# A Conformer layer on one core: the first feed-forward part and the input projection of four token tiles laid between the attention steps of the four others

## What is computed

```
x = x + 0.5 * SwiGLU_1(RMSNorm(x))
h = RMSNorm(x); z = h @ w_in                        # 2500 columns: queries, keys, values, indexer
group A: differential attention, 4 heads, two softmaxes per head, p0 - lam * p1, 128-wide values
group B: 8 query heads over one shared key and value head; a 4-head indexer scores all keys,
         the 256 best of each query are kept (top_k), and attended
x = x + concat(A, B) @ w_out
x = x + 0.5 * SwiGLU_2(RMSNorm(x))
outputs: x of prompt and sample, and the new keys and values of both
```

## Time and profile before

| | us |
|---|---|
| median of 3 executions | 2976.89 (2973.33 to 2980.42) |
| the profiled execution | 2983.27 |
| its span | 2981.5 |
| TensorE busy | 2581.9 (87%) |
| VectorE busy | 1353.0 (45%) |
| ScalarE busy | 858.9 (29%) |
| GpSimd busy | 127.4 (4%) |
| DMA | 74 GB/s in the mean |

### The profile page before, as it was taken

The page is one execution under the profiler, slowest core; times in us unless marked ns, Lnnn a source line. Parts: engine busy times, 40 slices in busy tenths (PEclk is TensorE's granted clock), DMA queues, the critical chain, the costliest instruction groups (busy, mean ns, idle before and its releaser), DMA issues. The chain is left out here.

```text
span 2981.5 us, 35915 instructions
## 1 busy us (share of the span) xinstructions
PE 2581.9 (87%) x13666; PEld 2273.2 (76%) x13666; DVE 1353.0 (45%) x2724; ACT 858.9 (29%) x1431; POOL 127.4 (4%) x191
## 2 busy tenths in 40 slices
PE   5999999999987997357788678888999877999998
PEld 4999999999986886236565567677778666988998
DVE  5333333333325422487443377887655323444343
ACT  3111111111113111354311355653333213222221
POOL 1000000000002211001000000110000000000000
PEclk8999999999998999556889789999999988999999
DMA  5111111111002213511531623332222132221220
GB/s 184 41 43 42 43 42 43 44 42 42 5 20 94 106 43 91 186 39 43 158 107 43 176 78 92 95 85 73 71 68 60 48 126 92 84 84 42 84 84 35
DMA packets 197714, 222.02 MB, mean 74 GB/s; under 512 B 29392, under 2 KB 158192, under 8 KB 196720
## 3 DMA queue, kind: packets, MB, share of 16 engines
q1 hardware_dynamic: 196528, 211.34, 22.6%
q10 hardware_dynamic: 1088, 9.44, 0.8%
HBM read 177.79 MB, written 32.74 MB: 71 GB/s over the span
## 5 line engine op out<-in xcount | busy, mean ns | idle before, releaser
L506 PE MATMUL a_bank<-XTh_a,f_gu_hi 128*128 128x384 f32 x1056 | 353.7, 335 | 3.0 <-DVEq L487 3.0
L508 PE MATMUL a_bank<-XTh_a,f_gu_lo 128*128 128x384 f32 x1056 | 353.4, 335 | 0.0
L507 PE MATMUL a_bank<-XTl_a,f_gu_hi 128*128 128x384 f32 x1056 | 353.3, 335 | 0.0
L471 DVE TENSOR_TENSOR f_hid<-f_silu,a_bank 128x384 f32<-128x384 f32 x66 | 36.6, 554 | 420.3 <-ACT f_silu L443 420.3
L506 PE MATMUL b_bank<-XTh_b,f_gu_hi 128*128 128x320 f32 x704 | 218.3, 310 | 3.0 <-DVEq L487 3.0
L508 PE MATMUL b_bank<-XTh_b,f_gu_lo 128*128 128x320 f32 x704 | 218.2, 310 | 0.0
L507 PE MATMUL b_bank<-XTl_b,f_gu_hi 128*128 128x320 f32 x704 | 218.1, 310 | 0.0
L506 PEld LDWEIGHTS a_bank<-XTh_a,f_gu_hi 128*128 128x128 f32 x1056 | 198.8, 188 | 3.8 <-DVEq L487 3.4
L507 PEld LDWEIGHTS a_bank<-XTl_a,f_gu_hi 128*128 128x128 f32 x1056 | 198.8, 188 | 0.4
L508 PEld LDWEIGHTS a_bank<-XTh_a,f_gu_lo 128*128 128x128 f32 x1056 | 198.7, 188 | 0.0
L443 ACT ACTIVATE f_silu<-a_bank 128x384 f32<-128x384 f32 x66 | 32.5, 492 | 449.1 <-PE a_bank L508 449.1
(11 more groups left out here) (392 smaller groups left out, 5638.0 us busy)
## 6 DMA issues: line engine op xcount, KB each, us to landing
f_gu_raw<-in_w_gate SPq DMA_DIRECT2D x22, 1024.0 KB, 5.5
f_gu_raw<-in_w_up SPq DMA_DIRECT2D x22, 1024.0 KB, 8.0
f_d_raw<-in_w_down SPq DMA_DIRECT2D x22, 1024.0 KB, 5.5
h_w_raw<-in_w_gate SPq DMA_DIRECT2D x22, 512.0 KB, 4.0
h_w_raw<-in_w_up SPq DMA_DIRECT2D x22, 512.0 KB, 5.3
h_w_raw<-in_w_down SPq DMA_DIRECT2D x11, 1024.0 KB, 4.9
win_w_raw<-in_w_in SPq DMA_DIRECT2D x4, 2048.0 KB, 8.6
s_k_in<-in_cache_diff_k SPq DMA_DIRECT2D x8, 1024.0 KB, 5.4
```

Of the source, the lines that this page charges most:

```text
L471: dve.tensor_tensor(hid[:, n % 2], silu[:, n % 2], psum[2 * (n % 2) + 1][:, 0:TOK_CHUNK], ALU.mult).then_inc(gated, 1)
L506: pe.matmul(out, hi, XTh[:, k, tok], start=(k == 0), stop=False)
L507: pe.matmul(out, hi, XTl[:, k, tok], start=False, stop=False)
L508: last = pe.matmul(out, lo, XTh[:, k, tok], start=False, stop=(k == KD - 1))
```

## The change

Tiles 0 to 3 and the sample (`FIRST`) go through steps 1 to 3 alone. The feed-forward part runs over five tiles in chunks of 320 tokens and stores its result rows to `x_scr`, which now has room for all nine tiles; the stage waits for the stores. `project_in` has five banks. `prepare` is called twice, once for each half of the tiles, and stores the transposed keys (and, the first time, the near table) itself, waiting for the stores.

`late_half` becomes a general function `merged` (L904) with two modes. With "out" it does what it did, but loads x of tiles 0 to 3 (four transfers of 512 KB) from `x_scr`. With "in" it takes the place of `early_attention`: the attention of tiles 0 to 3 is laid against the norm, first feed-forward part, second norm and input projection of tiles 4 to 7. Its dense units are 4 for the norm (steps 0 to 3), 132 for the feed-forward part (4 to 135), 4 for the second norm (136 to 139), and 40 for the projection (140 to 179), each of 24 matmuls 256 wide, with four result banks: those of gate, up and the two results. Its attention steps are 8 of the indexer (only tiles 2 and 3 have more than 256 keys) and two for each of 32 + 32 passes, up to about step 152; search rounds lie in steps 8 to 62. The scores of one pass fit in one bank, so two passes have one each. One tile is counted by VectorE, one by ScalarE. Between steps about 152 and 179 only the projection is left. The new order is: `FIRST` through steps 1 to 3, `prepare` early, `merged` "in", `sample_attention`, `prepare` late, `merged` "out", and step 8 as before.

The core of the diff (`merged` is new as a function, and most of it is the text of `late_half`; a few of its lines follow as they stand):

```diff
-                for t in range(NP):
+                for t in EARLY:
                     sp.dma_start(X[t], io["x_prompt"][0, t * P:(t + 1) * P, :]).then_inc(loaded, 16)
...
-    BANKS, SLOTS = 6, 4
+    BANKS, SLOTS = 5, 4
...
+                sp.wait_ge(copied_a, 2 * NP)
+                sp.wait_ge(copied_v, NP)
+                cols = slice(first * P, (first + NP) * P)
+                sp.dma_start(key_scr[:, 0:2 * DIFF_HEADS, cols], dkS.bitcast(F32)[:]).then_inc(kept, 16)
+                sp.dma_start(key_scr[:, 2 * DIFF_HEADS:, cols], keep["skikS"].bitcast(F32)[:]).then_inc(kept, 16)
+                if tables:
+                    sp.wait_ge(hidden_set, 1)
+                    sp.dma_start(near_scr, near[:]).then_inc(kept, 16)
+                sp.wait_ge(kept, 48 if tables else 32)
...
+def merged(nc, io, tag, mode, TILES, ATT, iw, q_gain, nlam, sub_gain, ident, q_scr, key_scr, near_scr, o_scr, x_scr):
+    N_OUT = D // GROUP if mode == "out" else 0
+    N_IN = -(-IN_COLS // GROUP) if mode == "in" else 0
+    BANKS_IN, LAG = 4, 2
+    U_OUT = NE if mode == "out" else 0
+    U_NORM = U_OUT + N_OUT * NE
+    U_PAIR = U_NORM + NE
+    U_NORM2 = U_PAIR + 12 * N_PAIR
+    U_IN = U_NORM2 + (NE if mode == "in" else 0)
+    N_UNITS = U_IN + N_IN * NE
...
+    SEARCHED = [t for t in ATT if (t + 1) * P > TOPK]
+    S_SLOTS = 2 if LMAX <= 512 else 1
...
+                def load_x(t):
+                    tok = slice(TILES[t] * P, (TILES[t] + 1) * P)
+                    sp.dma_start(XA[:, t, :], x_scr[tok, :] if mode == "out" else io["x_prompt"][0, tok, :]).then_inc(x_loaded[t], 16)
...
+                if mode == "out":
+                    sp.dma_start(gain_b[0], io["g_ffn2"].to_broadcast([P, D])).then_inc(gain_loaded, 16)
+                    for t in range(NE):
+                        load_x(t)
...
+                double(0)
...
+                    else:
+                        c, t = divmod(k - U_IN, NE)
+                        n = k - U_IN
+                        if t == 0:
+                            pe.wait_ge(lo_split, C_IN + c + 1)
...
+                        if n >= BANKS_IN:
+                            pe.wait_ge(in_taken, n - BANKS_IN + 1)
+                        wide = in_width(C_IN + c)
+                        project(in_bank[n % BANKS_IN][:, 0:wide], C_IN + c, t, wide, in_done)
...
+            half_ffn(nc, "f1", X, FIRST, 320, XTh, XTl, io["w1_gate"], io["w1_up"], io["w1_down"], psum, norm("n1", io["g_ffn1"]), kept)
+            project_in(nc, io, FIRST, XTh, XTl, iw, q_scr, psum, norm("n2", io["g_mix"]))
+        prepared("ke", EARLY, near_scr)
+        merged(nc, io, "m", "in", LATE, EARLY, iw, q_gain, nlam, sub_gain, ident, q_scr, key_scr, near_scr, o_scr, x_scr)
...
+        prepared("kl", LATE, None)
+        merged(nc, io, "h", "out", EARLY, LATE, iw, q_gain, nlam, sub_gain, ident, q_scr, key_scr, near_scr, o_scr, x_scr)
```

2069 lines of the change are left out of this document (857 added, 1212 removed).

## The result

The changed kernel takes 2987.43 us (median of 7, 2984.61 to 2988.42), the kernel before 2975.38 (median of 7, 2971.53 to 2980.42; three of the seven are those shown ahead of the prediction). The ratio is 1.0038, 95% interval 1.0026 to 1.0050: slower by about 12 us. The prediction was 2975, a difference of −2.2. The changed kernel was not run again as it is; in the comparisons further down the kernel before has medians of 2977.25 to 2979.49, against which 2987.43 is 8 to 10 us slower. The profiled execution of the changed kernel took 2984.61, its span is 2982.8.

A forecast was written before the change was run, and what follows sets the result against it. Dense stages were taken as bound by TensorE matmuls, early attention by chained waits with 108 us of TensorE idle. Merged stage +431.3 against savings led by −335.6 and −106.8 summed to −2.2: median 2975 us, range 2940 to 3012.

The forecast's parts named there:

- Stage m: Merged stage of early attention with tiles 4 to 7's dense work: 662 us in place of 230.7, +431.3.
- The +1 for the sample's start: Sample's attention, otherwise unchanged: 1 us more for starting colder.
- I take two thirds of it: 4.6: Stage m's five search pairs: TensorE stall of 4.6 us from the late half's 6.7, so 43 a pair.
- With the same stall 42.6: Stage m's six sparse pairs: tile 4's stall of 2.5 us kept, so 42.6 a pair, 256 in all.
- 13 us of marks and lower clock: Stage m's feed-forward pairs: 13 us added for marking chosen keys and stretches at the lower clock.
- The preparation, −0.2: First key preparation: about 10 us saved by four key tiles, offset by waited stores of 4.2 MB; −0.2 us in all.
- Weights are loaded and split a second time, +21: First feed-forward part divided in two: four tiles' dense work costs 361 us beside 340 when done together, +21.
- the wait at the late start: Late half's start: x loads ahead of the query doubling delay the first score, +6 us, between 0 and 10.
- B: Stage m overlaps better: stalls about 1.4 us a pair, pairs 39.9 and 41.4, kernel 2945 us; chance 0.32.
- C: Stage m slower: VectorE behind in down units, 6.3 us a pair, pairs 46 and 45.5, kernel 3010; 0.32 with D.
- D: Stage m without overlap: attention waits for split weights, some 706 us, +44; counted with C, together 0.32.
- The forecast's own test: Stage m under 640 or over 690 us would mean the forecast is wrong in its main step.

The follow-up runs named there:

- second trace of before: The kernel before, unchanged, profiled a second time: 2977.3 us, span 2975.5.
- the other order of loads: Changed kernel, stage m loading indexer queries and keys ahead of x and gains, late half loading x last: 2985.57 us, ratio 1.0019 to before.
- the edited down unit: Changed kernel, both merged stages: each pair's first down unit multiplies the first hidden block before waiting for the second: 2963.98 us, ratio 0.9946 to before.
- the two fastest forms: Both kernels with first hidden block early in merged and five-tile parts; changed also with loads reordered, before with stores later: 2925.08 and 2932.36 us.

## Why the prediction was wrong

**The comparison with one trace.** The difference was worked out against an execution of 2983.27 us and put on a median of 2976.89. That execution was 7.9 above the median of the seven, and the changed kernel's profiled one 2.8 below its own; of the 12 us between the medians the two profiles show 1.3. The forecast of 2974.7 missed 2987.43 by 12.7 us: 6.4 are the step from the profiled execution to the median, which the prediction named and let pass, 2.8 the changed kernel's own profiled execution, and only 3.5 the sum of the stages (a span of 2979.3 forecast, 2982.8 measured). The second trace of before shows where an execution varies: in the attention, the sample and the start of the late half. This error is of the size of the effect.

The 3.5 us are small by luck. Stage m took 11.4 more than forecast and the first preparation 4.2 more; the sample and the late half took 3.5 and 3.6 less, most of the other stages up to 1.3 less each. The second trace of before has the sample at 198.9 and the late half at 743.5, so more than half of what these two gave was the first trace standing high. The +1 for the sample's start is shown by no run: in the changed kernel the sample took 198.4 us, in the second trace of before 198.9.

**The size of the stalls in the pairs.** The failed step is "I take two thirds of it: 4.6" and "With the same stall 42.6". It scaled a wait with VectorE's load. Measured, TensorE idles 495.0 − 446.3 = 48.8 us in the pairs (5.3 a pair in the search pairs, 3.7 in the six others), where 5 × 4.6 + 6 × 2.5 = 38 were forecast: all of the 11 us by which they were missed. The stall that was scaled is made of other waits. In the three search pairs of the earlier trace rows it is these two and 3.0 us for an attention output, and none is for the product of gate and up:

```profile
PE h_turned L1981 <- ACT h_pT L2092: 8.6, 5, 3.4
PE h_result L1945 <- DVE XA L2198: 8.3, 6, 2.0
```

In stage m the largest part, 19.5 us, is that chain, half of it in the search pairs, and but for 2.3 us in the first pair it does not change with VectorE's load. The earlier trace rows had it in the idle time of tile 4's pair (1.75 us, 1.5 of them this wait) and of tile 7's (0.9, all of it), and the prediction took the first for a constant and the second for none, where the attention's matmuls cover a chain of one length. Shorter attention steps cover less of it. The dose of cover (19.5, 12.8, 6.6 us with none, three and six matmuls) shows this. For 13 us of marks and lower clock, TensorE's busy time came out 13.7 above 432.6, so that term held.

**The preparation, −0.2.** It is 32.2 us to stage m's first matmul, forecast 28. SP waits for the keys to be copied and only then stores; the last store, of the near table, is waited for at the end:

```profile
SPq L819 <- DMA near_scr<-ke_near: 9.7, 1, 9.7
```

The stores hid beside nothing: the first is issued at 725.1, behind the last copy, and stage m's first load follows at 738.5. But part of the 32.2 is not preparation. The four loads of x stand ahead of the queries that stage m's first matmul needs. With the queries first (the other order of loads) the stretch took 24.2 us and the start behind it 34.3. The prediction had x under the start, 28 and 36; measured are 32.2 and 30.4, 62.6 against 64 for both.

**A right sum with a wrong reason.** "Weights are loaded and split a second time, +21" is 361 + 481 − 821, and the sum held. But TensorE's idle time in the five-tile part was 27.3 against 7.7, 16.8 of it the wait for the second hidden block, which the earlier trace rows already showed for the last part (485.90 with 464.31 busy). With the wait covered, the two parts lose 19.6 and 19.9 us.

**What held.** Preparation and start of stage m taken together, the stand-alone feed-forward part, norms, projection and second preparation, and in the main the wait at the late start (6 forecast, 4.0 to 4.7 measured), with the row that answers to the earlier trace rows:

```profile
PE h_scores L1533 <- DMA h_q_lo<-h_q_lo: 21.4, 2, 17.7
```

**The rivals.** B is out: no search pair fell to its 39.9 in any form, and a sparse pair to its 41.4 only with the edited down unit (39.8). Of C the price was nearer (45.0 against its 46 and 45.5), its mechanism wasn't: VectorE's additions cost 14.9 us in eleven pairs, 1.4 each and not 6.3. D is out: 673.4 us for stage m and not 706. By "Perfetto Trace Analysis", Optimization Strategy, of the Trainium skill, interleaving the regimes may improve performance. In the kernel as changed it did not; between the two fastest forms it did, by 7 us where 108 were idle.

The forecast's own test, 640 to 690 us for stage m, was passed with 673.4. It was too wide to find an error of 11 us where the whole was forecast at 2.

## What to carry to other kernels

Look at each place where TensorE turns from one kind of product to the next that needs its result by way of other engines: the chain has its own length (2.0 us here, for tiles of 128x512), and what matters is how many independent matmuls TensorE can do meanwhile. Splitting work into smaller groups shortens that cover and makes waits where there were none, in stages that the change seems only to shorten. A change that is forecast at a small difference of large terms is compared with several executions of the kernel before, and the waits of the old form are first taken out of both. When one trace stands for a kernel, first look how much a stage varies between traces of the same code.

## What the runs showed that was not expected

- Two of the best edits have nothing to do with the change. Stores of 9.4 MB issued just ahead of transfers of 64 KB, for which TensorE waits, cost 14.6 us; six matmuls moved ahead of a wait in each pair of its late half took the kernel before to a ratio of 0.9968.
- Stages agree between executions within 0.5 us when full of matmuls, while those that wait on transfers and other engines varied by 2 us between two traces of the same kernel. Between kernels with the same code there, the late half's first pair varied by 3 us, and stage m's five search pairs by 6 (218.1 and 224.1 us): there TensorE's busy time was 194.5 and 201.0 us at a granted clock of 0.98 and 0.95.
- A wait shown as "issue" was a wait for VectorE's result: once matmuls stood ahead of it, the view named the releaser. Why it did not before stays open.
- Each of the 11 waits of 1.5 us in a five-tile part gave back 1.8 us when it was covered (19.6 and 19.9 us for the parts).
